# A two-block layer stack: another order of attention and scan work, and another bank for half of a group norm's mean and variance

## The reference

```python
mu = jnp.mean(wkv, axis=-1, keepdims=True)
var = jnp.mean(jnp.square(wkv - mu), axis=-1, keepdims=True)
wkv = ((wkv - mu) * lax.rsqrt(var + RWKV_GN_EPS)).reshape(B, S, RWKV_WIDTH)
```

```python
y_a = gla_branch(...)    # 4 heads, gated linear scan in both directions
y_b = diff_branch(...)   # 4 heads: softmax(q0 k0) - lam * softmax(q1 k1), times v
y_c = hgrn_branch(...)   # 4 heads, the same scan with other gates
x = x + rms_norm_2(concat(y_a, y_b, y_c) @ w_out[layer], norm_post[layer])
```

## Time and profile before

| | |
|---|---|
| median of 3 runs | 4496.89 us |
| the profiled execution's own time | 4500.21 us |
| its span | 4498.4 us |
| mean granted TensorE clock | 0.931 |
| TensorE busy | 3923.6 us, 87% |
| VectorE busy | 1992.3 us, 44% |
| ScalarE busy | 1439.2 us, 32% |
| GpSimd busy | 958.7 us, 21% |

### The profile page before, as it was taken

One profiled execution on the slowest core, in us unless ns is written; L12 is line 12 of the kernel. 1 busy time (PEld: TensorE's weight loads), 2 busy tenths in 40 slices (PEclk: granted clock), 3 DMA queues, 4 the chain that ended last, 5 costly groups with the idle time before them and its releaser, 6 DMA issues.

```text
span 4498.4 us, 66792 instructions
## 1 busy us (share of the span) xinstructions
PE 3923.6 (87%) x29404; PEld 2409.6 (54%) x29404; DVE 1992.3 (44%) x2165; ACT 1439.2 (32%) x1795; POOL 958.7 (21%) x426
## 2 busy tenths in 40 slices
PE   6988899999989999988997978988787978978777
PEld 3555565666656665455444555555444455555444
DVE  2456455555454642432224354263642264264542
ACT  4222323233232322222113323333444232343442
POOL 2313333232333322031132201111002210111002
PEclk8999999999999999999998988989888989989899
DMA  2111111111111112432212000100012100100002
GB/s 92 53 39 39 48 39 53 39 53 45 43 50 42 57 49 84 159 122 103 104 69 86 30 10 19 33 15 24 19 52 76 34 10 10 43 19 20 24 8 101
DMA packets 61585, 226.93 MB, mean 50 GB/s; under 512 B 6832, under 2 KB 8560, under 8 KB 60784
## 3 DMA queue, kind: packets, MB, share of 16 engines
q1 hardware_dynamic: 50064, 181.77, 11.7%
q10 hardware_dynamic: 11232, 40.90, 2.3%
HBM read 174.93 MB, written 47.71 MB: 49 GB/s over the span
## 4 chain that ended last, share of the span: by engine, by line
PE 71%; DVE 16%; ACT 9%; DMA 2%; issue 1%; POOL 1%; ACTq 0%; DVEq 0%; SPq 0%; POOLq 0%
PE psum L955 69%; DVE arena L2038 6%; ACT arena L1524 5%; DVE arena L2041 4%; DVE arena L2493 2%; DVE arena L2430 2%; PE psum L958 2%; ACT L1524 1%; ACT wh L1524 1%; DMA arena<-in_w_proj_conv 1%; DVE arena L2045 1%; ACT arena L1979 1%; DVE hl L2038 0%; ACT hh L1524 0%; POOL wl L2548 0%
## 5 line engine op out<-in xcount | busy, mean ns | idle before, releaser
L955 PE MATMUL psum<-arena 64*64 64x32 f32 (+11 forms) x19116 | 1589.3, 283 | 390.4 <-ACT arena L1524 186.2
L955 PEld LDWEIGHTS psum<-arena 64*64 64x64 f32 (+5 forms) x19116 | 1109.5, 158 | 878.5 <-issue 448.8
L2548 POOL TENSOR_TENSOR wl<-arena,wh 128x1024 bf16<-128x1024 f32 (+1 forms) x195 | 474.7, 2434 | 2405.4 <-ACT wh L1524 2403.6
L955 PE MATMUL psum<-hh,wh 128*128 128x512 f32 x3120 | 891.4, 432 | 98.6 <-ACT arena L1524 24.7
L1524 ACT ACTIVATE arena<-psum 128x512 f32<-128x512 f32 (+4 forms) x660 | 415.8, 630 | 1393.7 <-PE psum L955 1055.3
L955 PE MATMUL psum<-hh,wl 128*128 128x512 bf16 x3120 | 784.0, 394 | 1.2 <-POOL wl L2548 1.2
L955 PEld LDWEIGHTS psum<-hh,wh 128*128 128x128 f32 x3120 | 607.0, 200 | 301.7 <-issue 58.6
L2038 DVE TENSOR_TENSOR arena<-psum,arena 128x512 f32<-128x512 f32 (+3 forms) x488 | 319.3, 654 | 973.7 <-PE psum L955 628.1
L955 PE MATMUL psum<-hl,wh 128*128 128x512 bf16 x3120 | 736.0, 383 | 5.6 <-POOL hl L2548 5.5
L2041 DVE SCALAR_TENSOR_TENSOR arena<-arena 128x1024 f32<-128x1024 f32 x356 | 573.9, 1612 | 83.1 <-ACT arena L1524 69.9
L2548 POOL TENSOR_TENSOR arena<-arena 128x1024 f32<-128x1024 f32 (+4 forms) x142 | 362.6, 2553 | 955.1 <-ACT arena L1524 467.9
(11 more groups left out here) (38 smaller groups left out, 834.1 us busy)
## 6 DMA issues: line engine op xcount, KB each, us to landing
arena<-in_w_in SPq DMA_DIRECT2D x161, 512.0 KB, 3.5
scr_g<-arena ACTq DMA_DIRECT2D x24, 512.0 KB, 2.6
arena<-scr_g SPq DMA_DIRECT2D x24, 512.0 KB, 4.4
arena<-in_w_out SPq DMA_DIRECT2D x24, 512.0 KB, 3.5
arena<-in_w_mem_kv SPq DMA_DIRECT2D x16, 512.0 KB, 3.5
scr_x<-arena SPq DMA_DIRECT2D x16, 512.0 KB, 3.6
arena<-scr_x SPq DMA_DIRECT2D x16, 512.0 KB, 7.4
arena<-in_x SPq DMA_DIRECT2D x8, 512.0 KB, 10.3
```

The costliest lines, as they stand in the source:

```text
L955: return pe.e.matmul(o, l, r, start=start, stop=stop)
L2548: return pool.seq.tensor_tensor(o, a, b, op)
```

## The change

Of the group norm's two means and two variances, the second half goes to bank 7 instead of the three banks of the solve. In `grow`, the key products come first, then the queries', then the tree's, and the next level waits for what it reads only. `dw` is split: `dr` (reciprocal and small product) stays with VectorE, the scaling goes to ScalarE as `e1`, and the combination `dw` is issued after the next block's `qk`. Main strand places may be short (one half-step of the fillers, not two). Levels and diagonals may take any bank between `dexp` and `dv`. Filler projections are given out in 16 parts of 3 matmuls, a part counting a quarter of a place. Copies out of a projection come half a place later (`copied`). The second layer's statistic takes an upper pair, the roots of `fin` and `pre0` change order, `consts2` waits for the other sum, at `small` one more weight tile is loaded ahead, and two of the final norm's steps come first. The paces are new.

```diff
@@ Filler, weave
-            self.owed -= 1
-                next(self.g)
+                self.owed -= next(self.g) or 1
...
+    for share in main:
+        for f, n in fillers:
+            f.step(n * (share or 1))
@@ chain
-            one(("gmean", ct, c), ("gmean", ct, c), SM)
+            one(("gmean", ct, c), ("gmean", ct, c), YB if c else SM)
...
-            one(("gvar", ct, c), ("gvar", ct, c), SM)
+            one(("gvar", ct, c), ("gvar", ct, c), YB if c else SM)
@@ closing
-        for t in tags[::-1]:
+        for t in tags:
             do("stat_sum", t)
             do("stat_end", t)
@@ levels, diagonals, copies
+    room = {"levels": LOWER}
+    def copied(g, key, *step):
+        yield from g
+        ps.keep(("proj", key), 2)
+        yield 0.5
+        do(*step)
+        ps.leave(("proj", key))
...
-                    held(("lev", L, t, lv, g, p), ("lev", L, t, lv, g, p))
+                    held(("lev", L, t, lv, g, p), ("lev", L, t, lv, g, p), room["levels"])
@@ dv_ready, and likewise qk_ready and head_out
-        yield from P(("dvp", L, h), A["w_in_2"][L][14 + h], f"p{L}", deep=4)
-        do("dv_copy", L, h)
-        yield
+        key = ("dvp", L, h)
+        yield from copied(P(key, A["w_in_2"][L][14 + h], f"p{L}", deep=1, share=0.25), key, "dv_copy", L, h)
+        yield 0.5
@@ attend (the new order)
+        if n < 32:
+            for c in range(2):
+                ps.take(("ds", L, h, q, c), 2, UPPER)
+                ps.keep(("ds", L, h, q, c), 2)
+            do("qk", L, h, q)
+        if n:
+            do("dw", L, *last)
+        yield True
+        (dmax of both maps)
+        yield True
+        (dexp of both maps, leave their banks, room["levels"] = ANY)
+            yield
+        (dt of the last block)
+            yield
+        (WT of the last block)
+        if n < 32:
+            do("dr", L, h, q)
+        yield
+        if n < 32:
+            do("e1", L, h, q)
+        (dv of the last block; room["levels"] = LOWER; yield; do; yield)
-    PACE = (0.6, 0.57, 0.54, 0.54)
+    PACE = (0.62, 0.59, 0.555, 0.555)
@@ mix
+        first.step(2)
...
-            for _ in attend(L, n):
-                ahead.step(pace[h])
-                other.step(BESIDE[h][q] / 6)
-                ahead.step(pace[h])
+            for short in attend(L, n):
+                for _ in range(1 if short else 2):
+                    ahead.step(pace[h])
+                    other.step(BESIDE[h][q] / 12)
@@ layers, loads
-            run(stat("pre1", S))
+            run(stat("pre1", S, UPPER))
-        fill(begun + 2)
+        fill(begun + (3 if s[0] == "small" else 2))
@@ waits of lev (TensorE) and xk (ScalarE)
-                    pe.wait_ge(*at("grow", L, t, lv - 1))
+                    pe.wait_ge(*at("grow_q", L, t, lv - 1, 1))
-                act.wait_ge(*at("grow", L, t, lv - 1))
+                act.wait_ge(*at("grow_k", L, t, lv - 1, 1))
@@ ScalarE, VectorE
+        def e1(L, h, q):
+            z = q % 2
+            act.wait_ge(*at("dr", L, h, q))
+            f(EX[z], EX[z], AF.Copy, scale=DST[:, 16 * z + 6:16 * z + 7]).then_inc(*act.up("e1", L, h, q))
...
-            ts(EX[z], EX[z], s[:, 6:7], None, MUL).then_inc(*dve.up("dw0", L, h, q))
```

More of the change, by code:

```diff
@@ L161, in weave @@
 def weave(main, *fillers):
-    for stage in main:
-        for f, *n in fillers:
-            f.step(n[min(stage or 0, len(n) - 1)])
+    for share in main:
+        for f, n in fillers:
+            f.step(n * (share or 1))
 def build(nc, ctx, A, out):
@@ L681, in build, with held @@
     do("consts2")
[L685 to L687 removed]
+    def held(step, use, among=LOWER):
+        ps.take(use, 2, among)
         ps.keep(use, 2)
         do(*step)
+    room = {"levels": LOWER}
[5 more added lines that the diff above has]
+        ps.leave(("proj", key))
     def scan(L):
```

75 lines of the change are left out of this document (40 added, 35 removed).

## The result

The changed kernel takes 4370.09 us (median of 4 runs, 4361.94 to 4379.58) where the kernel before, on the same chip, took 4494.99 us (4 runs, 4492.08 to 4504.83): a ratio of 0.9719, 95% interval 0.9694 to 0.9745. The forecast was 4394 us, faster; the range 4338 to 4468 holds the measured time. The likeliest case was right in sign and kind, at the edge of its own range (4370 to 4430): the time came out 24 us lower, and the saving by medians was 124.9 us where 103 were forecast. The profiled executions' spans differ by 128.2 us, and that is what is broken down here.

A forecast was written before the change was run, and what follows sets the result against it. TensorE, busy 87% of the span, was taken to bound the kernel through standstill and slow clock. 72 + 18 + 12 + 1 = 103 us off 4500.2 gives 4397, median 3.3 lower: 4394 us; range 4338 to 4468.

The forecast's parts named there:

- likeliest case: Whole kernel: all terms together give 4394 us, in 4370 to 4430; chance 0.50.
- first rival: Mixing layers give nothing because each stall has a second cause behind it: 4466 us; chance 0.18.
- (a): Mixing layers, order inside `grow`: levels start up to 2.5 us sooner at 18 changes; 22 us a layer, at most 45.
- (b): Mixing layers, attention's order, free banks, finer projection parts: less waiting for the masked copy; 10 us a layer, bounds 0 and 33.
- (c): Mixing layers, price of 32 scalings moved to ScalarE: costs 8 us a layer, bounds 0 and 34.
- slower rival: Mixing layers: transposes wait for the combination in all 64 blocks, 1.5 us a block, 4562 us; chance 0.06.
- (d): Mixing layers, TensorE's clock: slow time falls in proportion to standstill; 12 us a layer, granted clock 0.90 or more.
- (e): First block's loop, second halves of mean and variance in the eighth bank: no wait for ScalarE; 18 us, bounds 0 and 22.
- second rival: The variance wait moves to its neighbour, the next solve matmul, needing the same ScalarE copies: 4412 us; chance 0.12.
- (f): Start of second layer, statistic in upper banks: first projection starts 12.3 us sooner, bounds 8 and 13.
- (g): Start of first mixing layer, final norm's root ahead of the layer's: TensorE goes 1 us sooner, bounds -1 and 2.
- (h): Third weight tile and two final norms ahead, other PACE: 0 us, bounds 0 and 5; the 13.7 us stall stays.

The follow-up runs named there:

- b_grow: Kernel before with only the new order inside `grow` and the finer waits of level matmuls and copies: 4492.64 us, ratio 0.9986.
- a_alone: Kernel after with, in the mixing layers, only attention's order, short places and paces kept; old `grow`, lower banks, parts of 12, undelayed copies: 4457.78 us, ratio 0.9905.
- a_lower: Kernel after with levels and diagonals held to the lower banks 0 to 3: 4401.34 us, ratio 0.9776.
- a_coarse: Kernel after with filler projections in 4 parts of 12 matmuls again: 4357.17 us, ratio 0.9675.
- a_dve: Kernel after with the scaling back on VectorE at the place of `dr`, none on ScalarE: 4375.78 us, ratio 0.9713.
- a_best: Kernel after with filler projections in 4 parts of 12 and the final norm's steps spread beside the first head's projections: 4356.08 us, ratio 0.9676.
- b_pre1: Kernel before with only the second layer's statistic in an upper bank pair: 4486.76 us, ratio 0.9976.
- a_oldpace: Kernel after with both old tables, `PACE` and `BESIDE`, of the kernel before: 4403.32 us, ratio 0.9782.
- a_nodelay: Kernel after without the half-place delay of ScalarE's copies out of a projection: 4402.84 us, ratio 0.9781.
- a_first: Kernel after with the first block's final norm handed out four times slower beside the first head's projections: 4370.91 us, ratio 0.9704.

## Why the prediction was right, and where not

**The worth of a part depends on the others.** In the two layers, `grow` alone saves 2 to 6 us (b_grow) and the attention's order with the paces alone 8 to 12 (a_alone), while all together save 94. Taken back one at a time from the kernel after, they cost: `grow` 22, free banks 30, delayed copies 24, paces 28; the fine parts give back 16. For `grow` this is shown both ways, 2 to 6 against 22, and the groups say why: alone, its wait passes to the masked copy; with the rest it doesn't. My forecast had named this as the first rival ("each stall has a second cause behind it"), and it is right for `grow` alone.

It isn't the whole story. On top of the attention's order, `grow`, banks, delay and parts together bring 85 us (1975.2 to 1889.7), while taken back one at a time they cost 22 + 30 + 24 - 16 = 60. The likely reading, which no run tests, is that some of them also stand in for each other: with one gone, the rest still save part of what it saved. Banks, delay and paces were never added alone, and the attention's order was never taken back, so how the 94 us divide among the parts stays open.

(a) `grow`, forecast 22 us a layer. The mechanism is shown by the timeline (copies 1.50 instead of 3.88 us behind) and by the idle for ScalarE before the level groups, 48.4 to 8.5 us, well below the 26 forecast. Its worth is 11 us a layer within the change and 1 to 3 alone. The step that failed: I took half of the upper end for "where the copies of another bank end last" as if that half were sure; it is a quarter with the rest of the change and next to nothing without it.

(b) Attention, banks, parts, forecast 10 us a layer. The free banks are worth 15 a layer (a_lower). The idle for the masked copy fell to 17.3 and 18.0 us (forecast 23). The parts of three, which I counted to the gain, cost 8 a layer (a_coarse). That leaves 7 and what the attention's order brings, which no run shows by itself. Wrong in the list: the reciprocal still waits, 18.4 us where it was 28.6. `dr` stands only a place or two behind the exponential, which would explain it; no run tests that.

(c) The price, forecast 8 a layer: about nothing (a_dve), though VectorE's waits for the scaling (67.9 us) are in the trace. The transposes did gain a wait for the combination, the sign that I had named for the slower rival: 5.1 us a layer over 32 blocks, 0.16 us a block, a tenth of the 1.6 from which it would have decided.

(d) The clock, forecast 12 us a layer: the granted clock rose, 0.89 to 0.91 and 0.91 to 0.92 over the whole layers, 0.90 and 0.91 over the middle. TensorE was busy at the lower level for 21.6 and 7.7 us less (table under a_coarse). Half of that, 7 us a layer, is an estimate of what the clock returned; I had 12. The parts of 3 took most of it back: with the holes counted as busy, TensorE's busy time fell by 4.7 us in the first layer and rose by 0.9 in the second, so of the 53 and 41 us 48.3 and 41.7 are standstill. With parts of 12 the return is there: 21.0 and 9.2 us of busy time (a_best), where half of the time no longer spent at the lower level is 20.5 and 6.1.
The Trainium skill (TensorE: Matmul & The Clock Gate, What's actually happening) puts the ramp penalty below 1% of a typical kernel's span. These layers do not agree: the granted clock stayed at 0.89 to 0.92 in every kernel here.

(e) 18 us: measured 20.6 by medians, idle 22.0 to 0.0. Right, at the upper end. The variance wait did not move to its neighbour (second rival out).

(f) 12.3: measured 12.7 between the landmarks, 11.8 by b_pre1. Right.

(g) 1 us: TensorE's idle there is 6.87 for 7.90. Right, as far as one wait in one pair of traces shows.

(h) 0: the stall is there, 11.86 for 13.68 us. But "other PACE: 0" is the plainest error. I counted places handed out and wanted, found no shortage, and took that for no effect. Paces and distribution together are worth 14 us a layer (a_oldpace). The half-place delay of the copies, worth 12 a layer (a_nodelay), was in the diff and in no term at all.

So 36 a layer was forecast as 22 + 10 - 8 + 12. Measured were 53 and 41, and what each part costs when it is taken back is 11 (`grow`), 15 (banks), 12 (delay), 14 (paces) and -8 (parts), each with its share of the clock in it. The sum came near because terms that I had missed, delay and paces, replaced terms that I had over-priced, `grow` and clock; as a method of sizing it was lucky.

## What to carry to other kernels

Where a standstill has several causes that end within a microsecond of each other, the idle put down to one releaser is no estimate of what its removal brings: taken away alone it gave 1 to 3 us a layer of the 48 put down to it, and with the other causes gone 11. So test a part both ways, added alone and taken back from the whole, and look for the next releaser in the groups. And when parts are added up against a kernel that lacks several of them, list every one that it lacks: the sum for a_alone missed one, worth 28 us. Filler rates and the place at which a queue's slow step is issued are terms like any other; and finer interleaving of matmuls has a price in busy time that must be set against the standstill it fills. Before standstill and busy time of two traces are compared, compare the counts of matmuls and weight loads.

## What the runs showed that was not expected

TensorE's busy time in the two layers, less half of what it spent busy at the lower clock level, is the same to 4 us in seven kernels whose plans, standstill (240 to 324 us) and lengths (1873 to 1988 us) differ widely, and 10 us higher, the same to 6, in the seven with parts of three. The price of interleaving can be read from it where lengths scatter by 4 us and the printed clock has two digits.

The two mixing layers run the same plan but for the final norm's steps beside the first, and yet removing the same part gives different losses: without the free banks 16.6 and 13.9 us, without the new paces 13.9 and 13.7, without `grow` 8.1 and 13.7. Part of this can be scatter: a_first changed the second layer by 6.8 us without touching it.
